# Eight load buffers in place of four for the down projection of the experts, in a two-block model kernel on one Trainium2 core

## The reference, cut to what matters

```python
def peer_ffn(h, wq, keys, u_tab, v_tab):
    ...
        top, pos = lax.top_k(cand, PEER_TOPK)
        eidx = jnp.take_along_axis(cidx, pos, axis=-1)
        g = jax.nn.softmax(top, axis=-1).astype(ht.dtype)
        u = u_tab[eidx]
        v = v_tab[eidx]
        a = jax.nn.gelu(jnp.einsum('thkd,td->thk', u, ht))
        return jnp.einsum('thk,thkd->td', g * a, v)
```

## Time and profile before

| | us |
|---|---|
| median of 3 runs | 1440.28 |
| range | 1438.72 to 1440.81 |
| span of the profiled execution (first to last instruction) | 1428.6 |
| what lies around the span, against the median | 11.7 |
| PE busy in the span | 1394.3 (98%) |
| DVE, ACT, POOL busy | 1126.3, 771.0, 388.7 |
| moved by DMA | 363.40 MB |

### The profile page before, as it was taken

One profiled execution on the slowest core, in us unless ns is written; L12 is line 12 of the kernel. 1 busy time (PEld: TensorE's weight loads), 2 busy tenths in 40 slices (PEclk: granted clock), 3 DMA queues, 4 the chain that ended last, 5 costly groups with the idle time before them and its releaser, 6 DMA issues.

```text
span 1428.6 us, 28088 instructions
## 1 busy us (share of the span) xinstructions
PE 1394.3 (98%) x10819; PEld 1298.0 (91%) x10819; DVE 1126.3 (79%) x2293; ACT 771.0 (54%) x1580; POOL 388.7 (27%) x423
## 2 busy tenths in 40 slices
PE   9899999998999999999999999999999999999998
PEld 7678998878889988898899999999999999999998
DVE  5776996788668889867668997667777698899987
ACT  6875886753355555677553203233333456566665
POOL 7700001000200000001100124788777423234230
PEclk9999999999999999999999999999999999999999
DMA  7305554651469989753354699999999999999995
GB/s 267 95 18 185 177 177 144 196 177 48 164 222 343 317 322 342 255 168 99 121 162 149 213 379 343 372 351 362 374 354 358 326 358 340 336 340 345 357 336 185
DMA packets 100275, 363.40 MB, mean 254 GB/s; under 512 B 11169, under 2 KB 11297, under 8 KB 100017
## 3 DMA queue, kind: packets, MB, share of 16 engines
q1 hardware_dynamic: 68096, 245.71, 49.7%
q0 software_dynamic: 24272, 88.64, 17.3%
q10 hardware_dynamic: 7776, 27.27, 5.3%
HBM read 360.52 MB, written 1.05 MB: 253 GB/s over the span
## 4 chain that ended last, share of the span: by engine, by line
PE 75%; DMA 9%; DVE 9%; ACT 4%; issue 2%; POOL 1%; DVEq 0%; SPq 0%; ACTq 0%
PE ps L641 73%; DMA arena<-in_peer_v 7%; DVE w_lo L1383 4%; DVE arena L1383 2%; ACT w_hi L2303 2%; DVE arena L1389 2%; ACT arena L2300 1%; DMA arena<-in_peer_u 1%; DMA arena<-in_u_rows,arena 1%; PE ps L859 1%; POOL arena L3224 1%; POOL arena L3213 1%; PE ps L986 0%; DVE act_hi_lo L1383 0%; PE ps L816 0%
## 5 line engine op out<-in xcount | busy, mean ns | idle before, releaser
L1383 DVE TENSOR_TENSOR w_lo<-arena,w_hi 128x512 fp32r<-128x512 f32 x680 | 455.2, 689 | 157.8 <-ACT w_hi L2303 152.9
L2303 ACT ACTIVATE w_hi<-arena 128x512 fp32r<-128x512 f32 x680 | 415.6, 625 | 285.9 <-PE ps L641 214.7
L641 PE MATMUL ps<-act_hi_lo,w_hi 128*128 128x256 f32 (+1 forms) x2496 | 552.9, 314 | 8.5 <-DVE w_lo L1383 6.5
L641 PE MATMUL ps<-arena 128*128 128x176 f32 (+7 forms) x4780 | 478.3, 281 | 13.8 <-issue 3.8
L641 PEld LDWEIGHTS ps<-arena 128*128 128x128 f32 (+3 forms) x4780 | 452.3, 165 | 34.8 <-issue 16.5
L641 PE MATMUL ps<-act_hi_lo,w_lo 128*128 128x176 f32 (+1 forms) x1760 | 455.2, 259 | 0.1
L641 PEld LDWEIGHTS ps<-act_hi_lo,w_hi 128*128 128x128 f32 x2496 | 420.5, 190 | 16.5 <-ACT w_hi L2303 8.3
L641 PEld LDWEIGHTS ps<-act_hi_lo,w_lo 128*128 128x128 f32 x1760 | 335.8, 191 | 0.2 <-issue 0.2
L641 PE MATMUL ps<-w_hi,act_hi_lo 128*128 128x512 f32 (+2 forms) x960 | 301.2, 389 | 7.2 <-DVE w_lo L1383 3.2
L1383 DVE TENSOR_TENSOR arena<-arena 128x512 f32<-128x512 f32 (+18 forms) x308 | 184.0, 606 | 55.6 <-ACT arena L2300 49.6
L641 PEld LDWEIGHTS ps<-w_hi,act_hi_lo 128*128 128x128 f32 x960 | 179.3, 188 | 49.6 <-issue 10.4
(11 more groups left out here) (104 smaller groups left out, 671.2 us busy)
## 6 DMA issues: line engine op xcount, KB each, us to landing
arena<-in_w_ff SPq DMA_DIRECT2D x128, 512.0 KB
arena<-in_peer_u SPq DMA_DIRECT2D x128, 512.0 KB
arena<-in_peer_v SPq DMA_DIRECT2D x128, 512.0 KB
arena<-in_w_ada ACTq DMA_DIRECT2D x48, 512.0 KB, 5.3
arena<-in_w_glu SPq DMA_DIRECT2D x16, 512.0 KB
arena<-in_peer_wq SPq DMA_DIRECT2D x16, 512.0 KB
arena<-in_w_in SPq DMA_DIRECT2D x12, 512.0 KB
arena<-in_w_conv SPq DMA_DIRECT2D x12, 512.0 KB
```

Of the source, the lines that this page charges most:

```text
L641: return e.matmul(o, l, r, start=start, stop=stop)
L1383: return e.tensor_tensor(o, a, b, op)
L2303: return e.activation(o, a, ACT.Copy)
```

## The change

The 128 units of `peer_v` get eight buffers. Four are the ring as before, the other four lie at 23552 (a stretch of the arena that is free then), at `OFF_GB + 1024` (free behind the gate numbers), and at `OFF_HN` and `OFF_HN + 1024`, the two places of the one-hot rows. `raw_place` gives place, semaphore, count and the unit that must be used up before. Units 0 to 3 of every eight go to the new places, 4 to 7 to the ring. Nothing changes for the units ahead of `peer_v`, nor in the order of the loads.

```diff
+    first_v = next(i for i, x in enumerate(plan) if x[0] == "peer_v")
+    DEEP = (23552, OFF_GB + 1024, OFF_HN, OFF_HN + 1024)
+
+    def raw_place(i):
+
+        m = i - first_v
+        turn, k = divmod(m, NDEEP)
+        if m < 0:
+            return OFF_RING + (i % NRAW) * UNIT, ring_in[i % NRAW], i // NRAW + 1, i - NRAW
+        if k < NDEEP - NRAW:
+            return DEEP[k], deep_in[k], turn + 1, i - NDEEP if turn else None
+        r = (first_v + k) % NRAW
+        loaded = (first_v - 1 - r) // NRAW + 1
+        return OFF_RING + r * UNIT, ring_in[r], loaded + turn + 1, i - NDEEP if turn else first_v - NRAW + k % NRAW
...
-            before = i - NRAW
+            _, landed, _, before = raw_place(i)
             if i == 1:
                 e.wait_ge(x_in[1], 16)
-            if before >= 0 and plan[before][0] == "peer_u":
+            if i == first_v:
+                for s in (ND // 4 - 2, ND // 4 - 1):
+                    e.wait_ge(*mm_done["spread", s])
+            if before is not None and before >= 0 and plan[before][0] == "peer_u":
                 e.wait_ge(*u_done["unit", before - first_u])
-            elif before >= 0:
+            elif before is not None and before >= 0:
                 e.wait_ge(lo_cut.sem, last_cut[before] + 1)
-            e.dma_start(raw(i), source).then_inc(ring_in[i % NRAW], 16)
+            e.dma_start(raw(i), source).then_inc(landed, 16)
```

More of the change, by code:

```diff
@@ L19 @@
 NRAW = 4
+NDEEP = 8
 CUT = 512
@@ L159, in build_in @@
     ring_in = [sem(f"ring_in{i}") for i in range(NRAW)]
+    deep_in = [sem(f"deep_in{i}") for i in range(NDEEP - NRAW)]
     x_in = [sem(f"x_in{t}") for t in range(2)]
@@ L273, in build_in @@
     first_u = next(i for i, x in enumerate(plan) if x[0] == "peer_u")
+    first_v = next(i for i, x in enumerate(plan) if x[0] == "peer_v")
[10 more added lines that the diff above has]
+        return OFF_RING + r * UNIT, ring_in[r], loaded + turn + 1, i - NDEEP if turn else first_v - NRAW + k % NRAW
     def raw(i):
-        o = OFF_RING + (i % NRAW) * UNIT
+        o = raw_place(i)[0]
         return ar[:, o:o + plan[i][2]]
     def raw_in(i):
-        return ring_in[i % NRAW], 16 * (i // NRAW + 1)
+        _, landed, count, _ = raw_place(i)
+        return landed, 16 * count
     def raw_piece(n):
```

## The result

The changed kernel takes **1424.87 us** (median of 6 runs, 1422.56 to 1427.66), beside 1440.55 us for the kernel before (6 runs, 1438.18 to 1441.88). The ratio is 0.9908, with a 95% interval of 0.9888 to 0.9927: 13.3 us less, 10.5 to 16.1 (the two medians by themselves differ by 15.7 us). I had forecast 1432.8, with a range of 1430.0 to 1440.5. The profiled execution has a span of 1423.3 us; its time was 1425.08.

The account below looks back on a forecast made before the run. PE bounds the kernel, stalled 9.4 us in the down projection by late loads. With 1.9 us staying, 7.5 are gained: 1428.6 - 7.5 = 1421.1 us span, plus 11.7 to the median, 1432.8 us; range 1430.0 to 1440.5.

Parts of the forecast that it names:

- What bounds the kernel: Whole kernel: PE, busy for 98% of the span, sets the time; in the down projection it is stalled for 9.4 us.
- The turn of the ring against load and cutting: Down projection: four buffers turn in 8.7 us at PE's pace, but load (7.45 us) and cutting need 9.3 us.
- SP's 227.6 us of waiting: Loader queue, down projection: SP waited in 118 loads for DVE to return a buffer, read as showing the ring is the limit.
- What stays of the stalls: Down projection: 1.9 us of PE's 9.4 us of stalls remain, scaled up from 0.12 us in 18 us; gain 7.5 us.
- The sum: Whole kernel: profiled span 1428.6 less 7.5 is 1421.1; with 11.7 us of median over span, 1432.8 us.
- Gathers late: Rival, down projection: beside eight loads gathers take 17.3 us, at most 15.0 allowed, so DVE waits; 1449.8 us, chance 0.10.
- DMA full as it is: Rival, down projection: a DMA share of 0.95 is the ceiling; gain only 2.5 us, 1437.8 us, chance 0.17.
- DVE's order: Rival, down projection: PE really waits for DVE's order of work, not the load; gain 5 us, 1435.3 us, chance 0.14.
- Not doing what it says: Rival: SP is held at the spread, or eight loads are as late as four were; 1440.3 us, chance 0.04.
- The term of 0 for the earlier start: End of up projection: earlier `peer_v` loads delay the last `peer_u` load by 0 us, at most 1.4 us.
- The new wait for the spreads: Start of `peer_v` loads: the first load waits for the last two spreads, already done by then, costing 0 us.

Follow-up runs that it names:

- `b_again`: The kernel before (four buffers), nothing changed, run and profiled once more: the profiled execution took 1435.0 us.
- `three`: The changed kernel, but from the ninth unit of the down projection SP waits for the unit three before: 1500.22 us (1 run).
- `late`: The changed kernel, but the first four loads of the down projection wait for up-projection units 124 to 127 as before: 1425.78 us, ratio 0.9908.
- `five`: The changed kernel with five buffers for the down projection in place of eight: 1423.46 us (ratio 0.9881), once more 1424.75 us (0.9901).
- `six`: The changed kernel with six buffers for the down projection in place of eight: 1426.76 us, ratio 0.9912.
- `b_look4`: The kernel before (four buffers), nothing changed, profiled yet again: that execution took 1436.5 us.

## Why the prediction was right in kind and wrong in size

- **What bounds the kernel: right.** PE is the limit, it is stalled in the down projection, and the stalls come from late landings. The turn of the ring against load and cutting was the right sum with a wrong term: the 7.45 us that I took for the load was one of the slow ones, the median is 6.2 (`b_again`). So "9.3 us" is 8.2 for an undisturbed unit and about 8.3 on the mean of `three`, against 8.7: four buffers are on the edge and not beyond it.
- **A reading that proved nothing.** I took SP's 227.6 us of waiting as a sign of the limit. It is 219.9 us with eight buffers.
- **What stays of the stalls: mis-sized by 1.3 us.** I let 1.9 stay, 0.6 us did. The stretch from 1133 to 1151 that I scaled up was one of four buffers and held a late load of its own, 0.7 us of waiting.
- **The sum: the step that failed.** "The median of the runs lies 11.7 us over the span", which I carried over as a constant. The runs show that 1.8 us lie around a span, so 9.9 us of it was the difference between a quick execution and the usual one. Of these, 3.4 us are the usual start of the stage, which is as late with the change. The rest goes with the change: 2.1 us are stalls of the down projection beyond those of that one profile, and 4.4 us no profile shows (last point). With the 1.3 us above they make 7.8 of the error of 7.9 us. Over nine profiles with four at a time the distance is 294.0 us on the mean, over six with five or more at full work (changed kernel twice, `late`, `five` twice, `six`) 283.1 to 283.3. That makes 10.9 us, against my 7.5. The starts of the stage are the same in both, 1133.4 and 1133.6 us on the mean. From these means the changed kernel would take 1133.6 + 283.1 + 6.6 + 1.8 = 1425.1 us, and it does.
- **What stays open.** By the same sum the kernel before would take 1133.4 + 294.0 + 6.6 + 1.8 = 1435.8, and its medians are 1437.4 to 1440.6. The 10.9 us lie in the interval of the measured gain (10.5 to 16.1), at its lower end. The other 2 to 5 us I could not place. Chance in which executions were profiled is an unlikely reason: the nine profiled ones with four at a time took 1435.9 us on the mean (the first of them by its span) and the 85 other runs of these kernels 1439.3, three standard errors apart, while with five to eight, or without the gathers, the 8 profiled ones took 1425.5 and the 33 others 1425.4. The extra time lies inside the span, since time less span is 1.8 or 1.9 us in all of them, and only kernels with the short ring have it. That it is more of the same stalls is likely and not shown: of the other runs only span and mean clock are known.
- **Gathers late: out** (idle 0.0 before all 58 passes; 7.7 us to landing where 15.0 were to be had). **DMA full as it is: out**, 353 GB/s were reached, and 396 for 25 us. **DVE's order: out**, DVE was busy for 233.91 of 250 us and PE had no idle time. **Not doing what it says: out**, the landing waits are gone. The term of 0 for the earlier start holds too: the changed kernel and `late`, which starts nothing earlier, agree in time and in distance. The new wait for the spreads cost nothing: the first loads of the down projection start 0.12 us after the last load of the up projection has been issued (1121.63 + 2.71 = 1124.34 and 1124.46). Timeline of the SP queue of the changed kernel, the answer to the earlier trace rows:

```profile
1121.63 2.71 SPq L651 DMA_DIRECT2D arena<-in_peer_u  x2
1124.46 4.65 SPq L651 DMA_DIRECT2D arena<-in_peer_v  x6
```

## What to carry to other kernels

A ring of buffers must turn slower than a transfer with its processing takes, with room for the slow transfers. Weigh the turn (buffers times the pace of the limiting engine) against the usual time from issue to free, and not against one late load. Here the two were within a tenth of each other, 8.7 and about 8.3 us; one more buffer took the stalls away, and more beyond it gave nothing. Look at who waits for landings, not at how long the loader waits for places. And before the span of one profile is set against a median of runs, ask what lies around it: a difference much greater than the time less span of the same run means that the profile is of another execution than the usual one, and its stalls need not be the usual ones.

## What the runs showed of the hardware

Much of the scatter of the runs comes with the short ring: kernels with four at a time range over 1432.0 to 1447.5 us (93 runs, standard deviation 3.3), those with five to eight, or without the gathers, over 1420.6 to 1430.7 (41 runs, 2.1). Fixing a stall that sits on an edge took out part of the variance too.

In `three` a pause of PE cost nearly twice its length. No matmul started between 1279.61 and 1282.95, 3.1 us of it idle. From 1282 to 1289 the granted clock was 0.53, the level of 1.2 GHz most of the time, and the pairs came every 0.51 us in place of 0.271: the eleven from 1282.95 to 1288.59 took 5.6 us in place of 3.0. Windows of `three`, columns as before, and PE in it:

```profile
1276.00:1282.00 6.00, 3.85 (x29) 3.64 (x27) 2.41 (x3) 0.96 (x3) 1.14 (x1) 0.98 0.95 343
1282.00:1289.00 7.00, 6.05 (x25) 6.08 (x26) 5.76 (x9) 3.67 (x8) 1.75 (x1) 0.53 0.58 187
1289.00:1295.00 6.00, 6.00 (x46) 6.00 (x45) 5.19 (x9) 4.07 (x7) 1.15 (x1) 1.00 0.77 264
```

```profile
1285.55 0.56 PE L664 MATMUL ps<-act_hi_lo,w_hi 128*128 128x352 f32 x1
...
1286.06 0.56 PE L664 MATMUL ps<-act_hi_lo,w_hi 128*128 128x352 f32 x1
...
1286.57 0.56 PE L664 MATMUL ps<-act_hi_lo,w_hi 128*128 128x352 f32 x1
```

With four at a time the longest distance between pairs, beside the small matmuls, was 1.99 us (`b_look4`, from 1192.42), and the granted clock was 1.00 from 1150 to 1400 in all nine profiles, so the clock has no part in their stalls.
